# Two additions of a group's outputs on GpSimd instead of VectorE, in a decoder layer on one Trainium2 core

## What is computed

```
h = x * (1 + sc1) + sh1
x = layer_norm(ALPHA * x + g1 * mixer(h), ln1_g, ln1_b)
h2 = x * (1 + sc2) + sh2
f = square(relu(h2 @ w_up)) @ w_down          # 1024 -> 4096 -> 1024
x = layer_norm(ALPHA * x + g2 * f, ln2_g, ln2_b)
```

## Time and profile before

| | us |
|---|---|
| three runs | 2093.06, 2097.32, 2099.24 |
| median | 2097.32 |
| the profiled execution | 2099.51 |
| its span, first to last instruction | 2097.6 |
| TensorE, VectorE, ScalarE, GpSimd busy | 2044.4, 1436.7, 908.0, 1440.9 |

### The profile page before, as it was taken

One profiled execution on the slowest core, in us unless ns is written; L12 is line 12 of the kernel. 1 busy time (PEld: TensorE's weight loads), 2 busy tenths in 40 slices (PEclk: granted clock), 3 DMA queues, 4 the chain that ended last, 5 costly groups with the idle time before them and its releaser, 6 DMA issues.

```text
span 2097.6 us, 27969 instructions
## 1 busy us (share of the span) xinstructions
PE 2044.4 (97%) x10451; PEld 1713.2 (82%) x10451; DVE 1436.7 (68%) x1875; ACT 908.0 (43%) x1306; POOL 1440.9 (69%) x1101
## 2 busy tenths in 40 slices
PE   7899999999999999999999999999999999999996
PEld 5677887888997888888878888878888889999994
DVE  2455687696675545677887667788757777765686
ACT  2324213222213654545564554565444645444441
POOL 3345787874343677788878778887788866666672
PEclk9999999999999999999999999999999999999998
DMA  8796798873432455545445645544654534454341
GB/s 272 220 299 225 229 278 235 233 249 95 151 104 91 157 173 162 181 145 164 141 141 179 208 156 164 167 131 131 222 190 141 175 111 122 146 180 143 120 141 45
DMA packets 319953, 357.50 MB, mean 170 GB/s; under 512 B 12357, under 2 KB 251970, under 8 KB 319819
## 3 DMA queue, kind: packets, MB, share of 16 engines
q1 hardware_dynamic: 319818, 355.72, 54.4%
HBM read 321.22 MB, written 34.44 MB: 170 GB/s over the span
## 4 chain that ended last, share of the span: by engine, by line
PE 70%; DVE 8%; ACT 1%; POOL 1%; issue 1%; DVEq 0%; ACTq 0%
PE ps L1184 23%; PE ps L1186 22%; PE ps L1185 22%; PE ps L1448 1%; POOL w_hilo L897 1%; DVE hid_b L1911 1%; PE ps L1520 0%; DVE pair_sums L1933 0%; DVE pair_sums L1934 0%; DVE pair_sums L1930 0%; DVE htmp L1788 0%; DVE hid_a L1911 0%; DVE pair_sums L1929 0%; DVE mix L1628 0%; DVE acc L1783 0%
## 5 line engine op out<-in xcount | busy, mean ns | idle before, releaser
L897 POOL TENSOR_TENSOR w_hilo<-w_raw,w_hilo 128x512 fp32r<-128x512 f32 x890 | 1281.2, 1469 | 595.3 <-ACT w_hilo L978 594.5
L978 ACT ACTIVATE w_hilo<-w_raw 128x1024 fp32r<-128x1024 f32 x445 | 470.4, 1058 | 535.7 <-PE ps L1186 412.0
L1184 PE MATMUL ps<-hA,w_hilo 128*128 128x512 f32 (+1 forms) x1760 | 622.5, 354 | 9.3 <-ACT htmp L1054 4.1
L1185 PE MATMUL ps<-hA,w_hilo 128*128 128x512 f32 (+1 forms) x1760 | 620.3, 352 | 0.0
L1186 PE MATMUL ps<-hA,w_hilo 128*128 128x512 f32 (+1 forms) x1760 | 620.1, 352 | 0.0
L1184 PEld LDWEIGHTS ps<-hA,w_hilo 128*128 128x128 f32 x1760 | 332.0, 189 | 55.1 <-issue 8.4
L1185 PEld LDWEIGHTS ps<-hA,w_hilo 128*128 128x128 f32 x1760 | 332.0, 189 | 41.8
L1186 PEld LDWEIGHTS ps<-hA,w_hilo 128*128 128x128 f32 x1760 | 332.0, 189 | 41.5
L2007 DVE TENSOR_TENSOR acc<-acc,ps 128x512 f32<-128x512 f32 x270 | 177.9, 685 | 70.9 <-PE ps L1186 67.9
L1184 PE MATMUL ps<-w_hilo,hid_a 128*128 128x512 f32 x450 | 181.0, 402 | 1.7 <-ACT more_sums L1154 1.7
L1929 DVE TENSOR_TENSOR pair_sums<-htmp 128x256 f32<-128x256 f32 x62 | 36.2, 584 | 207.8 <-ACT htmp L1057 207.5
(11 more groups left out here) (239 smaller groups left out, 2830.4 us busy)
## 6 DMA issues: line engine op xcount, KB each, us to landing
w_raw<-in_w_up SPq DMA_DIRECT2D x128, 512.0 KB, 4.1
w_raw<-w_mix SPq DMA_DIRECT2D x124, 512.0 KB, 3.3
w_raw<-in_w_down SPq DMA_DIRECT2D x97, 512.0 KB, 3.8
w_raw<-in_w_in SPq DMA_DIRECT2D x64, 512.0 KB, 5.0
xt<-in_w_ada SPq DMA_DIRECT2D x20, 1024.0 KB, 8.4
w_raw<-in_w_out SPq DMA_DIRECT2D x32, 512.0 KB, 4.7
xt<-x_norm SPq DMA_DIRECT2D x19, 512.0 KB, 5.7
xt<-in_w_down SPq DMA_DIRECT2D x36, 256.0 KB, 5.0
```

Of the source, the lines that this page charges most:

```text
L897: ins = pool.tensor_tensor(W[:, g % SLOTS, 1, cols], raw[:, g % RAW, cols], W[:, g % SLOTS, 0, cols], ALU.subtract)
L978: act.activation(W[:, g % SLOTS, 0, :], raw[:, g % RAW, :], ACT.Copy).then_inc(hi_done, 1)
L1184: pe.matmul(out, w_hi, x_hi, start=start, stop=False)
L1185: pe.matmul(out, w_hi, x_lo, start=False, stop=False)
```

## The change

GpSimd makes the two additions for tiles 0 and 1 of a group's outputs, at each of the three boundaries, in four parts of 128x512: both tiles' right halves (m5 += m7) behind its low part of U(b, 2), and both left halves (m4 += m7) behind that of U(b, 3). Ahead of the first it waits until the group's last product is summed (`d_evac`) and VectorE has done step 4 (`sums_ready` at 2s+1). The last of the four raises `sums_ready` to 2s+2. VectorE's steps 5 and 6 for these boundaries are gone; the last group keeps its own.

```diff
+            def add_sums(s, part):
+
+                if part == 0:
+                    pool.wait_ge(d_evac, sums_done(BLOCKS * s + BLOCKS - 1, 6, 1))
+                    pool.wait_ge(sums_ready, 2 * s + 1)
+                for t in range(2):
+                    a = acc[:, t, HALF:] if part == 0 else acc[:, t, 0:HALF]
+                    ins = pool.tensor_tensor(a, a, more_sums[:, 1, HALF * t:HALF * t + HALF], ALU.add)
+                    if part == 0 or t == 0:
+                        step(ins)
+                if part == 1:
+                    ins.then_inc(sums_ready, 1)
...
-            gate_after = {}
+            gate_after, sums_after = {}, {}
             for s in range(SUPERS - 1):
                 b = BLOCKS * s + BLOCKS
+                sums_after[SLAB["U", b, 2]] = (s, 0)
+                sums_after[SLAB["U", b, 3]] = (s, 1)
                 gate_after[SLAB["U", b + 1, 0]] = [(s, 3), (s, 2)]
                 gate_after[SLAB["U", b + 1, 2]] = [(s, 1), (s, 0)]
...
+                if g in sums_after:
+                    add_sums(*sums_after[g])
                 for s, t in gate_after.get(g, []):
...
-            def end_of_group(s, i):
-
-                if i < 2:
-                    outputs(s, [5 + i])
-
...
-                if kind == "U" and s and r == 0:
-                    end_of_group(s - 1, i)
```

## The result

The changed kernel takes 2098.69 us, the median of 20 runs (2094.51 to 2102.96). The kernel before, in 20 runs of its own, takes 2094.83 (2092.37 to 2099.24). The ratio is 1.0018, with a 95% interval from 1.0011 to 1.0024: some 3.9 us slower, between 2.3 and 5.0. That is a small loss, less than 0.3%, and nothing is won.

What follows compares the result with a forecast made beforehand. TensorE, busy 97%, was taken to bound the kernel; GpSimd's lag would add 2.1 + 2.1 + 0 = +4.2 us at the three boundaries, giving 2101.5 us on the median of 2097.32, range 2094 to 2107.

Steps and rivals of the forecast that it cites:

- The first residual: VectorE's first residual at each of the first two boundaries: 1.23 us before, forecast at about 2.2.
- the third wait: TensorE's wait at the third boundary, 4.13 us before: forecast between 2.7 and 5.5 us.
- the added wait of GpSimd: GpSimd's new wait behind U(8,2)'s low part until VectorE's step 4 is done: forecast to cost neither queue anything.
- the turns: First two boundaries: five VectorE turns cost GpSimd 3.1 us, less 1.0 for L2034: net +2.1 us at each.
- Nobody waits for L2032: VectorE's removed addition L2032, said to stand in idle time, with nobody waiting for it.
- TensorE's wait in front of U(9,3): TensorE's last wait at the first boundary: forecast between 1.5 and 3 us, put down to GpSimd's low part.
- the 3.9 us that I expected TensorE to wait: TensorE's forecast waiting at a boundary, in pieces, given under the rival of a slower clock.
- Hidden: Rival: the additions fill GpSimd's 7.7 us of idle time and VectorE's turns cause no delay; 2097.3 us, chance 0.20.
- Faster: Rival: VectorE's chain begins 1.25 us sooner, TensorE's small waits go, -1.8 us at two boundaries; 2093.7 us, chance 0.08.
- The lock in full: Rival: turns cost their full instruction lengths, 3.0 us at each of two boundaries; 2103.3 us, chance 0.08.
- Slower, by the clock: Rival: waits run together, half clock costs 1.7 more at two boundaries, third wait grows 1.4; 2106.3 us, chance 0.15.
- The third boundary: Boundary with longer slabs and much idle GpSimd: additions fit, the wait stays; 0 us, from -1.4 to +1.4.

Runs made afterwards that it cites:

- late_adds: The changed kernel with GpSimd's two pairs of additions one slab later, behind its low parts of U(b,3) and U(b+1,0); ratio 0.9997 to the kernel before.
- relief_only: The kernel before without VectorE's steps 5 and 6 at the three boundaries, on any engine, so some outputs lack terms; ratio 0.9981.
- early_steps: The kernel before with VectorE making step 6 right behind step 5, in U(b,0), both additions staying on VectorE; ratio 0.9996.
- wait_only: The kernel before with GpSimd's new wait behind its low part of U(b,2) and nothing else; VectorE keeps steps 5 and 6; ratio 1.0007.
- double_adds: The changed kernel with each of GpSimd's four additions at a boundary made twice; ratio 1.0103 to the kernel before.
- gates10_late: The kernel before with GpSimd's gates of tiles 1 and 0 moved behind its low part of U(b+1,3), their residuals later too; ratio 1.0025.
- gates_late: The kernel before with gates of tiles 1 and 0 behind U(b+1,3) and those of tiles 3 and 2 behind U(b+1,1); ratio 1.0024.
- late_adds_gates: The changed kernel with its additions one slab later and the gates of all four tiles late; ratio 1.0035 to the kernel before.

## Why the prediction came out as it did

**Sign and mechanism held, the size by the timed runs too.** Forecast was +4.2 us over the run of before; measured is +3.9 by the timed runs (2.3 to 5.0) and +2.4 by the matmuls of one profiled execution. By the matmuls the forecast is 1.8 us too high, so that it lies within 0.3 us of the timed difference is in part luck. The absolute time came out 2.8 us below the 2101.5 of the forecast. Nearly all of that, 2.5 us, is the base: the median of three runs was 2097.32, that of twenty is 2094.83.

**Step by step, with 5.69 added to the changed kernel's times.** The additions were to start at 1018.05: 1012.41 + 5.69 = 1018.10. No idle time was to follow: there are 0.25 us. U(9,3)'s low part was to end at 1068.4: it ended at 1061.92 + 5.69 = 1067.6, where before it was 1066.27. So GpSimd lags by 1.3 us, not by 2.1, and TensorE by 1.3. The first residual was to take 2.2 (2.21), the pair sums some 1.4 (they stand at 1.39 to 1.52), the third wait 2.7 to 5.5 (3.98). TensorE waits for no up slab of the group but U(9,3), so the added wait of GpSimd costs nothing in this kernel beyond the low part that it displaces, which is in the sum.

**The term that was mis-sized is the turns, +2.1 at a boundary where the trace gives +1.3.** The step that went wrong is that L2032 was put at nothing ("Nobody waits for L2032"). VectorE's addition at 1020.40 did meet GpSimd's next instruction. GpSimd's timeline of the kernel before, the first half of U(9,0)'s low part:

```profile
1020.86 1.91 POOL L897 TENSOR_TENSOR w_hilo<-w_raw,w_hilo 128x512 fp32r<-128x512 f32 x1 [4.22 <-ACT w_hilo L978]
```

It took 1.91 us instead of 1.29, so L2032 had cost a turn of 0.6, and that is gone as well. In the earlier trace rows this shows as 3.15 for a pair that takes 2.55 alone: I had the row and did not ask what stood in it. 2.1 less 0.6 is 1.5, within 0.2 of what was measured. Two more differences cancel, which is luck. The 1024-wide subtraction that now stands at 1026.15 costs GpSimd a turn of 1.0 which I had not counted, since GpSimd used to fall idle while it ran; and one of the residuals, with its turn of 1.0, has slipped behind the low part of U(9,3).

**One wait or four.** I expected TensorE's wait in front of U(9,3), between 1.5 and 3 us. It is 0.60 there, and three more stand in front of K(8,1), K(8,3) and K(8,4). That sign missed. So did the 3.9 us that I expected TensorE to wait at a boundary in all: the four pieces are 2.36. A lag of the helper is paid at the first slab whose cover is thin, and what was paid isn't paid again.

**The rivals.** *Hidden* is excluded by the interval, and by late_adds, which shows what hidden looks like. *Faster* had its mechanism right: the relief is worth 0.8 to 1.9 us at a boundary (relief_only), but GpSimd's lag outweighs it, as the prediction said it would. *The lock in full* has the turns too dear: the Trainium skill ("SBUF — State Buffer", section "Who interferes with whom") lets the loser block fully, for the whole instruction. By the page the lag would have been 3.0 us; it is 1.3, and early_steps has a pair of low parts 1.6 us longer than the 2.55 of a lone one while two additions with 2.4 us of work of their own stood beside it. This case's trace agrees with the page that each of the two engines waits for the other, and not on the full length: a 1024-wide instruction of VectorE, 1.23 us alone, costs GpSimd 1.0. *Slower, by the clock* did not come about in the changed kernel. Its longest wait at the first two boundaries is 0.85, and the granted clock there stays at 1.00. But the point from which I let that rival decide, a wait near 4.13 us, was too high: half clock follows one of 1.82. Windows of wait_only, behind a wait of 1.82 us at the second boundary, and of double_adds, behind the one of 3.42:

```profile
1387.43 0.47 PE L1189 MATMUL ps<-w_hilo,hid_a 128*128 128x512 f32 x1 [1.82 <-ACT more_sums L1159]
```

```profile
1388.00:1391.40 3.40, 3.40 (x10) 2.65 (x9) 3.33 (x3) 3.17 (x5) 3.40 (x3) 0.51 0.23 65
```

```profile
1040.50:1043.50 3.00, 3.00 (x8) 2.37 (x9) 1.64 (x2) 0.04 (x1) 3.00 (x3) 0.56 0.52 175
```

Both are at half speed, 1.2 GHz, for about as long as the stretch of the earlier trace rows. Not every such wait has it behind it (the last section has two that don't), so a wait's length alone doesn't decide. The chance of that rival should have been larger than I gave it: two of my experiments, gates10_late and gates_late, ran into it at all of the boundaries.

**The third boundary** came out at -0.2 where 0 was forecast.

## What to carry over

An engine that is 70% busy can be 100% busy in the stretch that matters. Before work is given to a helper, add up its instructions, its idle time and the turns that the other engine takes from it, over that stretch alone and to its end; when the idle time is used up, each further us is one of the engine that bounds. Where two engines share operands in SBUF, look first at what runs beside the other's chain: moving gates and an addition out of its way, all on their own engines, won about twice what moving work across engines lost. And look at the granted clock behind each long wait before its cost is put down to an engine: a boundary's figure moved by 1.0 to 1.4 us with it here.

## What the runs showed of the chip

- A single wait of TensorE of 1.82 us was followed by 3.4 us at half clock (wait_only). Waits of 1.0 and 1.5 in the same kernel were not, nor were four waits of 0.36 to 0.83 within 14 us. Nor does the length of the wait alone decide: behind one of 2.57 us (double_adds, the first row) and one of 2.76 us (late_adds_gates, third boundary, the second row) the granted clock stays at 1.00, behind one of 2.46 us (gates_late, third boundary) it falls. Where it falls, TensorE loses between 1.5 and 3.1 us by it, and behind the same wait of 4.13 us it lost 1.7, 2.7 and 3.1 us in three kernels.

```profile
1031.10:1034.50 3.40, 3.40 (x15) 2.83 (x16) 3.33 (x4) 0.00 (x0) 3.40 (x3) 1.00 0.53 154
```

```profile
1704.60:1710.20 5.60, 5.60 (x43) 5.60 (x44) 5.43 (x6) 2.69 (x6) 4.19 (x3) 1.00 0.00 0
```

- An instruction of GpSimd that waits for the one before it on the same engine costs about 0.1 us more: the two additions from 1012.41 to 1015.16 come every 1.37 us, the two low parts from 1015.16 to 1017.72 every 1.28.
- Where an instruction of VectorE and one of GpSimd start within 0.02 us of each other, either can come first, and a 1.22 us instruction takes 1.22 or 2.37 us by it (step 6 in the kernel before and in wait_only). TensorE's wait behind it grew by 0.7 us at the first boundary and 1.0 at the second.
- Beside VectorE's instructions of 1.23, 0.69 and 0.42 us, one of GpSimd's, 1.29 us alone, takes 2.27, 1.74 and 1.47 in the traces of before and of the changed kernel. So it is delayed by 0.98, 0.45 and 0.18: each time the length of VectorE's instruction less some 0.24.
